# Eight of twelve query/key pairs per layer as seven half-size block products, with sums made by VectorE

## The reference, cut to what matters

```python
for layer in range(DEPTH):                       # 2 layers
    h = rms_norm(x, norm_g[layer])
    p = h @ w_in[layer]                          # 1024 -> all projections
    c_q, c_kv, k_r, gate_a, dil_qkv, gate_b = jnp.split(p, split_points, axis=-1)
    a = mla_attention(c_q, c_kv, k_r, ...) * jax.nn.silu(gate_a)
    b = dilated_attention(dil_qkv, cos_d, sin_d) * jax.nn.silu(gate_b)
    x = x + jnp.concatenate([a, b], axis=-1) @ w_out[layer]
# dilated_attention: 3 groups (dilations 1, 4, 16), 8 heads of 64, for each group
    q = partial_rope(qkv[:, :, g, 0], cos, sin)  # the first 16 of 64 columns are turned
    k = partial_rope(qkv[:, :, g, 1], cos, sin)
    v = qkv[:, :, g, 2]
```

## Time and profile before

| what | value |
|---|---|
| median of three runs | 2022.21 us (2019.87 to 2025.78) |
| profiled execution | 2023.61 us, its span 2022.0 us |
| PE busy | 1977.7 us (98%) |
| DVE, ACT, POOL busy | 750.9, 561.8, 731.3 us |
| granted TensorE clock, mean | 0.995 |
| first block | about 0 to 1127 us |
| POOL's loop | 38 to 983 us, `ys` issued at 986.3 us |

### The profile page before, as it was taken

How to read it: one execution, slowest core, us unless ns; L and a number is a source line. 1 busy time by engine, 2 the same in 40 slices (tenths; PEclk the granted TensorE clock), 3 DMA queues, 4 the chain that set the end, 5 groups by cost and what they waited for, 6 DMA issues and landing times.

```text
span 2022.0 us, 28519 instructions
## 1 busy us (share of the span) xinstructions
PE 1977.7 (98%) x10560; PEld 1193.9 (59%) x10560; DVE 750.9 (37%) x1628; ACT 561.8 (28%) x1227; POOL 731.3 (36%) x1057
## 2 busy tenths in 40 slices
PE   9999999999999999999999999999999899989999
PEld 6544556655455455566554556547887444448886
DVE  1344443343112344433464637435222411444223
ACT  3234342215121443422152216422111311122110
POOL 1757576757575667676400121001100100001001
PEclk9999999999999999999999999998999999999999
DMA  7332434243354434332754220108996621139995
GB/s 289 113 123 81 139 127 154 69 180 120 114 196 146 162 106 138 125 132 90 280 227 167 78 83 1 64 32 321 375 365 231 242 83 42 63 132 359 364 367 209
DMA packets 74035, 338.03 MB, mean 167 GB/s; under 512 B 8712, under 2 KB 11206, under 8 KB 59334
## 3 DMA queue, kind: packets, MB, share of 16 engines
q1 hardware_dynamic: 41688, 216.98, 29.0%
q0 software_dynamic: 27920, 103.82, 14.7%
q10 hardware_dynamic: 4320, 15.73, 1.9%
HBM read 292.47 MB, written 44.04 MB: 166 GB/s over the span
## 4 chain that ended last, share of the span: by engine, by line
PE 91%; DVE 4%; DMA 2%; issue 2%; ACT 1%; DVEq 1%; SPq 0%; POOL 0%; ACTq 0%; POOLq 0%
PE psA L464 25%; PE psA L1844 11%; PE psA L1728 9%; PE psA L456 9%; PE psA L1765 6%; PE psA L627 5%; PE psSO L1874 5%; PE psT L443 3%; PE psA L505 3%; PE psSO L534 3%; PE psSO L544 2%; PE psT L1839 1%; DVE pool_mem L2694 1%; PE psSO L565 1%; PE psSO L600 1%
## 5 line engine op out<-in xcount | busy, mean ns | idle before, releaser
L464 PE MATMUL psA<-gB,pool_mem 128*128 128x512 f32 x1024 | 455.3, 597 | 0.0
L464 PEld LDWEIGHTS psA<-gB,pool_mem 128*128 128x128 f32 x1024 | 189.5, 190 | 224.2 <-issue 224.2
L395 POOL TENSOR_TENSOR pool_mem<-pool_mem,cs 128x256 f32<-128x256 f32 x448 | 271.3, 640 | 126.6 <-DMA pool_mem<-in_mod_w 126.0
L399 POOL TENSOR_TENSOR pool_mem<-pool_mem 128x256 f32<-128x256 f32 x336 | 246.2, 762 | 30.2 <-issue 22.3
L1844 PE MATMUL psA<-pool_mem 128*128 128x128 f32 x1952 | 224.2, 275 | 0.0
L1844 PEld LDWEIGHTS psA<-pool_mem 128*128 128x128 f32 x1952 | 221.6, 192 | 1.9 <-issue 1.9
L1728 PE MATMUL psA<-pool_mem 128*128 128x512 f32 (+1 forms) x528 | 208.8, 554 | 5.8 <-DVE pool_mem L2298 2.3
L456 PE MATMUL psA<-pool_mem,gB 128*128 128x256 f32 (+2 forms) x768 | 189.6, 403 | 1.6 <-ACT gB L797 1.6
L456 PEld LDWEIGHTS psA<-pool_mem,gB 128*128 128x128 f32 x768 | 143.9, 190 | 43.5 <-issue 7.1
L1728 PEld LDWEIGHTS psA<-pool_mem 128*128 128x128 f32 x528 | 99.3, 190 | 109.4 <-issue 99.5
L1679 POOL DMA_INDIRECT pool_mem<-xs_scratch,idx x4 | 3.9, 968 | 361.9 <-DVE idx L2432 361.3
(11 more groups left out here) (329 smaller groups left out, 2435.8 us busy)
## 6 DMA issues: line engine op xcount, KB each, us to landing
pool_mem<-in_w_gu SPq DMA_DIRECT2D x32, 2048.0 KB, 9.8
pool_mem<-in_mod_w POOLq DMA_DIRECT2D x56, 1024.0 KB, 7.9
pool_mem<-in_w_dn SPq DMA_DIRECT2D x32, 1024.0 KB, 13.3
pool_mem<-in_w_qk SPq DMA_DIRECT2D x24, 1024.0 KB, 5.1
ys_scratch<-pool_mem ACTq DMA_DIRECT2D x30, 512.0 KB, 9.7
ys_scratch<-pool_mem POOLq DMA_DIRECT2D x1, 12288.0 KB, 44.5
pool_mem<-in_odd_w_in SPq DMA_DIRECT2D x5, 2048.0 KB, 13.9
pool_mem<-in_w_out SPq DMA_DIRECT2D x4, 2048.0 KB, 8.2
```

Source lines behind the costliest of these rows:

```text
L395: nc.gpsimd.tensor_tensor(wm[:, b, k], wm[:, b, k], c_all[:, k].to_broadcast([P, MCH]), ALU.mult)
L399: nc.gpsimd.tensor_tensor(wm[:, b, k], wm[:, b, k], wm[:, b, n + k], ALU.add)
L464: m = nc.tensor.matmul(psA[:, n % 2, :], w(i), src[:, k, :], start=(i == 0), stop=(i == len(ks) - 1))
```

## The change

Eight pairs per layer, `SETS` (numbered `s` = 0 to 7), are no longer two tiles of 8 matmuls with 512 tokens. The product of weights (query and key columns, features low and high) and tokens (features low and high, early 256 and late 256 tokens) is a product of 2x2 blocks, made by seven block products instead of eight, each 4 matmuls of 256 tokens. The sums that this takes are made by DVE: once per layer four sums of the tokens (`hsum`, in the place of `x`), for each pair four sums of 128x512 weights (two into `wsum`, two into the weights' own place), and one sum or copy of 128x256 for each bank, eight per pair, to put the results together. The rotation now reads the tile from SBUF, no longer from PSUM: shuffle, product with the cosines, product with the sines, sum. The three pairs of `hp` = 0 and the pair (1, 0) stay as they were. `PA` goes from 88 to 128 projections. `x` is overwritten by the token sums, so SP loads it again in both layers (2 MB), behind the last pair's products; before, only layer 1 loaded it again, and earlier.

```diff
+    hsum = by(at(X_AT, 4096), 4, KD // 2)
+    wsum = by(at(W_AT + 2048, 2048), 2, 2, KD // 2)
...
@@ SP
-                if L + 1 == DEPTH:
-                    sp.wait_ge(x_stored, 16 * NT)
-                    for t in range(NT):
-                        sp.dma_start(x[:, t, :], d["x1"][t * P:(t + 1) * P, :]).then_inc(x_in_order, 16)
...
                 load(OUT_SLOT[0], d["w_out"][L, 0], KD * 512)
+                sp.wait_ge(pa_ready, base + pa_qk(3, 2, 1) + 1)
+                for t in range(NT):
+                    if L + 1 < DEPTH:
+                        sp.dma_start(x[:, t, :], d["x"][t]).then_inc(x_again, 16)
+                    else:
+                        sp.dma_start(x[:, t, :], d["x1"][t * P:(t + 1) * P, :]).then_inc(x_in_order, 16)
...
@@ PE
+            def project_set(L, s, parts):
...
+                products = ((w[:, low, tile(0)], hT[:, low, early]), (a[:, 1], b[:, 1]), (w[:, high, tile(0)], hT[:, high, early]),
+                            (w[:, low, tile(1)], b[:, 2]), (w[:, high, tile(1)], b[:, 3]), (a[:, 0], b[:, 0]),
+                            (w[:, high, tile(0)], hT[:, high, late]))
+                for i in parts:
...
+                    elif i == 1:
+                        pe.wait_ge(sums_ready, SUMS * L + 2 * s + 2)
+                    elif i == 6:
+                        pe.wait_ge(sums_ready, SUMS * L + 2 * s + 3)
+                    bank_free(n)
+                    weights, moving = products[i]
+                    for k in range(KD // 2):
+                        m = nc.tensor.matmul(psA[:, n % 2, 0:2 * P], weights[:, k, :], moving[:, k, :],
+                                             start=(k == 0), stop=(k == KD // 2 - 1))
+                    m.then_inc(pa_ready, 1)
...
                         elif hp:
-                            project_qk(L, hp + 1, t, 0)
+                            project_set(L, 3 * hp - 1 + t, range(0, 3))
...
                             if hp and not (hp == 2 and t == 2):
-                                project_qk(L, hp + 1, t, 1)
+                                project_set(L, 3 * hp - 1 + t, range(3, 7))
...
@@ DVE
+            def tokens_summed(L):
...
+                nc.vector.tensor_tensor(hsum[:, 0], hT[:, low, late], hT[:, low, early], ALU.subtract)
+                nc.vector.tensor_tensor(hsum[:, 2], hT[:, high, late], hT[:, low, late], ALU.subtract)
+                dve.drain()
+                nc.vector.tensor_tensor(hsum[:, 1], hT[:, high, late], hsum[:, 0], ALU.subtract)
+                dve.drain()
+                nc.vector.tensor_tensor(hsum[:, 3], hT[:, high, early], hsum[:, 1], ALU.subtract).then_inc(sums_ready, 1)
...
+            def weights_summed(L, s, which):
...
+                if which == 0:
+                    dve.wait_ge(w_loaded[loaded], 16 * (LOADS[loaded] * L + count))
+                    nc.vector.tensor_tensor(both, a21, a22, ALU.add)
+                elif which == 1:
+                    nc.vector.tensor_tensor(a21, a11, a21, ALU.subtract)
+                elif which == 2:
+                    nc.vector.tensor_tensor(less, both, a11, ALU.subtract).then_inc(sums_ready, 1)
+                else:
+                    nc.vector.tensor_tensor(a12, a12, less, ALU.subtract).then_inc(sums_ready, 1)
...
+            def set_out(L, s, i):
...
+                if i == 0:
+                    m = nc.vector.tensor_copy(k[:, early], bank)
+                elif i == 1:
+                    m = nc.vector.tensor_tensor(q[:, late], k[:, early], bank, ALU.add)
...
+            def set_rotated(s, c):
...
+                nc.vector.stream_shuffle(swapped[:], out, SWAP)
+                dve.drain()
+                nc.vector.tensor_tensor(out, out, ropeD[:, 0, :], ALU.mult)
+                rotated(*SETS[s], c)
```

More of the change, by code:

```diff
@@ L201, in pa_qk, with part_of @@
     def pa_qk(hp, g, c):
-        return PA_QK[hp][g][c] if hp else PA_MLA[g] + 4 * c
+        if (hp, g) in SETS:
+            assert c == 1
+            return part_of(SETS.index((hp, g)), 6)
+        return PA_QK1[c] if hp else PA_MLA[g] + 4 * c
+    def part_of(s, i):
+        return SET_LOW[s] + i if i < 3 else SET_HIGH[s] + i - 3
     def pa_v(hp, t):
@@ new lines, in weights_of @@
+            def weights_of(s):
+                slot, at, loaded, count = QK_SLOT[SETS[s][0]][SETS[s][1]]
+                w = eighths(slot, at, 2 * P)
+                low, high = slice(0, KD // 2), slice(KD // 2, KD)
+                return w[:, low, tile(0)], w[:, high, tile(0)], w[:, low, tile(1)], w[:, high, tile(1)], loaded, count
+            def weights_summed(L, s, which):
+                a11, a12, a21, a22, loaded, count = weights_of(s)
+                both, less = wsum[:, s % 2, 0], wsum[:, s % 2, 1]
+                dve.drain()
[8 more added lines that the diff above has]
+                    nc.vector.tensor_tensor(a12, a12, less, ALU.subtract).then_inc(sums_ready, 1)
@@ new lines, in set_out @@
+            def set_out(L, s, i):
+                hp, g = SETS[s]
+                q, k = qk_out(hp, g, 0), qk_out(hp, g, 1)
+                early, late = slice(0, 2 * P), slice(2 * P, S)
+                n = PA * L + part_of(s, i)
+                bank = psA[:, n % 2, 0:2 * P]
+                dve.drain()
+                dve.wait_ge(pa_ready, n + 1)
+                if i == 0:
+                    m = nc.vector.tensor_copy(k[:, early], bank)
+                elif i == 1:
+                    m = nc.vector.tensor_tensor(q[:, late], k[:, early], bank, ALU.add)
+                elif i == 2:
+                    m = nc.vector.tensor_tensor(q[:, early], k[:, early], bank, ALU.add)
+                elif i == 3:
+                    m = nc.vector.tensor_tensor(k[:, late], q[:, late], bank, ALU.add)
+                elif i == 4:
+                    m = nc.vector.tensor_tensor(k[:, early], k[:, late], bank, ALU.add)
+                elif i == 5:
+                    nc.vector.tensor_tensor(k[:, late], k[:, late], bank, ALU.add)
+                    m = nc.vector.tensor_tensor(q[:, late], q[:, late], bank, ALU.add)
+                else:
+                    m = nc.vector.tensor_tensor(q[:, late], q[:, late], bank, ALU.add)
+                m.then_inc(pa_copied[n % 2], 1)
@@ new lines, in set_low, with set_high @@
+            def set_low(L, s):
+                set_out(L, s, 0)
+                if s + 1 < len(SETS):
+                    weights_summed(L, s + 1, 0)
+                set_out(L, s, 1)
+                if s + 1 < len(SETS):
+                    weights_summed(L, s + 1, 1)
+                set_out(L, s, 2)
+                weights_summed(L, s, 3)
+            def set_high(L, s):
+                set_out(L, s, 3)
+                if s + 1 < len(SETS):
+                    weights_summed(L, s + 1, 2)
+                for i in (4, 5):
+                    set_out(L, s, i)
+                set_rotated(s, 1)
+                set_out(L, s, 6)
@@ L1138, in _ @@
                             queries_out(L, 2 * j + 3, n + 3)
-                        elif j == 3 and t != 2:
-                            rotated(1, t // 3, t % 3)
+                        elif j == 2 and t == 3:
+                            tokens_summed(L)
+                        elif j == 3 and t < 2:
+                            rotated(1, 0, t)
+                        elif j == 3 and t == 2:
+                            for which in range(3):
+                                weights_summed(L, 0, which)
                 for hp in range(4):
@@ L1188, in added @@
                     n = PA * L + PA_OUT + 2 * t + half
+                    if L + 1 < DEPTH and (t, half) == (0, 0):
+                        dve.wait_ge(x_again, 16 * NT)
                     dve.wait_ge(pa_ready, n + 1)
```

61 lines of the change are left out of this document (40 added, 21 removed).

## The result

The changed kernel took 2046.54 us in the median (2042.92 to 2048.59, 4 runs), the kernel before beside it 2022.71 us (2019.87 to 2025.78, 4 runs). The ratio is 1.0116, 95% interval [1.0094, 1.0137]: slower by 1.2%, 24 us. The forecast was 2055 us, range 2034 to 2076, with slower at 0.89. That the time came out in the range is in part luck: the profiled execution lost it elsewhere than forecast, as the next part shows. The profiled execution took 2042.92 us, its span 2040.9 us, 18.9 us above that of before.

A forecast was written before the change was run, and what follows sets the result against it. POOL's chain to the `ys` zeros was taken to bound alongside PE's: issue 29 us later, transfer 50 us, PE's values 30.3 us later, plus 3 of clock, 2023.6 + 33 = 2056.9; forecast 2055 us, range 2034 to 2076.

The forecast's parts named there:

- What PE gains: PE's projections of a pair: 12.1 us in place of 13.84, 1.75 us less, 28 us for 16 pairs in two layers.
- What it costs DVE: DVE's full steps: 17 to 19 us against PE's 18.3, so level; PE 1.5 us late in ten steps at most.
- reserve of 20 us and more: PE, ahead of its values in layer 1, `hp` 3, `t` 0: could lose 20 us and more before being last.
- What it costs POOL: POOL's products beside DVE operations with two SBUF operands: 112 x 0.26 = 29 us more, ends 21 and 38.
- nothing absorbs this time: POOL's turns: its added time moves its last issue in full, as loads start when stores are out; low end 15 us.
- The transfer of zeros: The zeros of `ys`, issued with 2.1 MB more of loads, take 50 us in place of 44.5; bounds 44.5 and 52.
- cost of nothing for the token sums and the reload of `x`: Four token sums per layer and layer 0's wait for the second `x`: nothing, hidden while PE is not last.
- rival 2: DVE is last, not POOL: ten full steps losing 6 us each, PE 32 us late, 2056 up to 2075; chance 0.08.
- PE waits there less than 20 us: Sign against the forecast, at layer 1, `hp` 3, `t` 0, where one PE wait of 40 us or more was expected.
- the forecast's mechanism: Layer 1, `hp` 3, `t` 0: POOL issues `ys` zeros late, DVE idles for them, PE stands 45 to 55 us; 0.70.
- Rival 4: Each added DVE operation in POOL's busy share costs POOL 0.69 us: 55 us late, time 2081; chance 0.11.
- the forecast's +33: PE's values in layer 1, `hp` 3, `t` 0, 30.3 us later, plus 3 us of low clock behind the wait.

The follow-up runs named there:

- gb_later: The changed kernel with SP's load of `w_gb` 0 and 1 moved behind the load of `w_v`; median 2053.2 us, ratio 1.0106 to the kernel before.
- two other edits: In the changed kernel, `w_gb` loaded behind `w_v` and the zeros of `ys` issued by ACT at the start of layer 1; 2030.5 us, 1.0026.
- gb_ys_short: Changed kernel, `w_gb` loaded behind `w_v`, zeros issued by ACT, the 64 weight sums over 8 elements in place of 512; 2039.1 us, 1.0069.

## Why the prediction was right, and where it was not

The direction, the range and most sizes held. The path by which the profiled execution got there was not the one I gave most weight, and that the time is still near the forecast is luck: two chains, POOL's and DVE's, arrived there together.

- **What PE gains.** Forecast 1.75 us a pair, measured 1.65 (21.83 to 20.18). Right.
- **What it costs DVE: the step that failed.** The copies on banks were as I took them (0.42 us against 0.45), and the sums of weights 0.69 to 1.2. But I compared DVE's work with PE's over a step (17 to 19 against 18.3) and let PE lose at most 1.5 us in ten steps, 15 us. It lost 31.6 in waits and 10.3 by the clock behind them, and the "reserve of 20 us and more" was used up. A sum over a step hides three things. DVE's work is a chain inside the step: PE's next product waits for one copy, and whatever stands before that copy in the queue counts (the sums at 271 us). It hides the tail: 5 us once is more than 1.5 us of shortfall. And it hides that behind each wait of 2 to 6 us PE ran some microseconds at half clock; I had counted one such stretch, 3 us, for my one long wait.
- **A load that a sum needs a step earlier than the product did.** I priced it not at all; it cost 4.9 us in layer 0 and 1.4 in layer 1. `gb_later` removes it.
- **What it costs POOL.** Forecast +29 us of arithmetic from 112 x 0.26. Measured +25.6 (284.1 + 254.7 + 46.7 against 271.3 + 246.2 + 42.4) in the changed kernel, +29.5 in `gb_later`. The term is right. The step behind it, *nothing absorbs this time*, is not: the last issue moved by +15.6, +7.5 and +38 us in three executions. In the changed kernel 14.2 us were absorbed in POOL's idle time ahead of its load issues (115.5 us on L422, 129.7 on L407 before). I had left the low end open to 15 us.
- **The transfer of zeros.** Forecast 50 us; 48.9, 48.6 and 49.2. Right, as was the cost of nothing for the token sums and the reload of `x`: no engine waited for either.
- **Forecast against rival 2.** I had said that I am wrong if PE waits there less than 20 us, or if the lost time is spread over the full steps. By that the forecast's mechanism was wrong for the profiled execution, and rival 2, *DVE is last*, with 0.08, was what happened: its 5.2 us instruction came twice, PE was 17.8 us late. Both mechanisms exist. With PE 11 us earlier and POOL 22 us later, `gb_later` waits 32.1 us for `ys`; without the zeros in POOL's hands the kernel still loses 0.75% of its 1.16%. They should have had about equal chances, since the time of the one is hidden under the other.
- **Rival 4, full exclusion.** The Trainium skill's page "SBUF — State Buffer", section "SBUF: two separate sides", lets such a pair exclude each other for a whole instruction. The measured 25.6 us disagree with the 55 it would cost POOL here. But on DVE's side it is not strong enough: a wait for one product of POOL would be 0.6 us, and DVE waited for seven or eight.
- **Two sums in the prediction.** DVE's terms add up to 16.5 to 19.5 us, not 17 to 19, and the forecast's +33 is 33.3 in the total. Neither changes the outcome.

## What to carry to other kernels

Work taken from the busiest engine and given to one that looks half idle is paid at the single instruction: read what stands in that engine's queue ahead of the thing the busy engine waits for, not its busy share. Here the change lost 1.2% with eight sets. With the two other edits in place it came to 1.0026 with eight, and to 0.9948 with four and the sums where DVE stood idle. Where two chains arrive together, price both before and after the edit, since relieving the first shows the second (as in `gb_later`).

## What the runs showed of the hardware

- A DVE instruction beside a row of POOL's eight products can be held until the row ends. It happens to small ones too, in the kernel with four sets to a copy of 16 columns, whose timelines of DVE and POOL start within 0.01 us of each other:

```profile
974.45 4.63 DVE L1166 COPY near_k<-near_k 128x16 f32<-128x16 f32 x1
```

```profile
974.45 4.60 POOL L414 TENSOR_TENSOR pool_mem<-pool_mem,cs 128x256 f32<-128x256 f32 x8
```

  It did not happen where a drain stood behind the row's first product, nor where there was one product only; but it did not happen with short sums of weights either (`gb_ys_short`), where the rows were whole. The held instructions at 847.89, 915.84 and 974.45 us start within 0.1 us of their rows. That alone does not decide. In the changed kernel, by the timelines of DVE and POOL, the two started together here as well, and DVE's instruction took its usual time:

```profile
780.44 0.69 DVE L1133 TENSOR_TENSOR pool_mem<-pool_mem,ropeD 128x512 f32<-128x512 f32 x1
```

```profile
780.44 5.60 POOL L410 TENSOR_TENSOR pool_mem<-pool_mem,cs 128x256 f32<-128x256 f32 x8
```

  And in the kernel with six sets an instruction was held that started 1.3 us into the row (timelines of DVE and POOL):

```profile
364.26 3.83 DVE L1154 TENSOR_TENSOR pool_mem<-pool_mem,ropeD 128x512 f32<-128x512 f32 x1
```

```profile
362.94 4.60 POOL L414 TENSOR_TENSOR pool_mem<-pool_mem,cs 128x256 f32<-128x256 f32 x8
```

  In these cases the row that holds DVE takes 4.60 us, eight products of 0.57, and the row that does not takes longer (5.60). What decides stays open.
- One more drain of POOL behind an instruction cost 2.25 us (126.0 / 56), in place of 0.6 for the product before it.
- The granted clock fell to 0.5 inside a long wait as well, 3.6 us after it began, and stayed there to its end. The table by stretch of the kernel with `w_gb` later, whose wait is from 1043.9 to 1076.0:

```profile
1042.60:1047.50 4.90, 1.30 (x29) 0.87 (x28) 0.00 (x0) 1.88 (x2) 0.00 (x0) 1.00 1.02 420
1047.50:1076.00 28.50, 0.03 (x2) 0.06 (x3) 2.29 (x4) 0.00 (x0) 0.00 (x0) 0.50 0.89 366
```
